# Expert layers of a two-block network on one core: overflow code out of line, transposes of half 0 ahead of the gate rows, one conditioning vector summed by column tiles

## The reference

```python
def layer_norm(x, g, b):
    mu = jnp.mean(x, -1, keepdims=True)
    var = jnp.mean(jnp.square(x - mu), -1, keepdims=True)
    return (x - mu) * lax.rsqrt(var + LN_EPS) * g + b
...
def moe_ffn(h, ...):            # 64 experts, 6 per token, one shared expert
    scores = jax.nn.sigmoid(xf @ router_w)
    ...                         # group-limited top 6, normalised gates topw
    routed = routed_experts(xf, topi, topw, w_gate, w_up, w_down)
    shared = (jax.nn.silu(xf @ sh_gate) * (xf @ sh_up)) @ sh_down
    return routed + shared
```

## Time and profile before

| | |
|---|---|
| time of three runs | 1858.17 us median (1858.16 to 1863.55) |
| the profiled execution: its own time, its span | 1860.38 us, 1858.6 us |
| mean granted TensorE clock in the span | 0.972 |
| busy: PE, PEld, DVE, ACT, POOL | 95%, 60%, 41%, 17%, 2% of the span |
| moved by DMA | 576.87 MB, mean 310 GB/s |

### The profile page before, as it was taken

One profiled execution on the slowest core, in us unless ns is written; L12 is line 12 of the kernel. 1 busy time (PEld: TensorE's weight loads), 2 busy tenths in 40 slices (PEclk: granted clock), 3 DMA queues, 4 the chain that ended last, 5 costly groups with the idle time before them and its releaser, 6 DMA issues.

```text
span 1858.6 us, 25707 instructions
## 1 busy us (share of the span) xinstructions
PE 1759.4 (95%) x10428; PEld 1109.3 (60%) x10428; DVE 756.0 (41%) x1545; ACT 307.6 (17%) x665; POOL 45.7 (2%) x86
## 2 busy tenths in 40 slices
PE   7999999999999979998999999999998699999998
PEld 3886754544444438887956544444443387778875
DVE  1667422222222225877764222222211366555173
ACT  1111300100000013431122101000000221320121
POOL 0110000000000000000000000000000000000000
PEclk7999899999999999999899999999999899999999
DMA  9978689999999975864386999999999765225301
GB/s 402 365 273 333 250 339 425 425 425 425 424 425 425 426 322 200 297 243 172 123 337 261 376 424 425 425 425 425 425 425 424 324 225 203 88 93 202 119 25 44
DMA packets 82099, 576.87 MB, mean 310 GB/s; under 512 B 9132, under 2 KB 11436, under 8 KB 12848
## 3 DMA queue, kind: packets, MB, share of 16 engines
q1 hardware_dynamic: 70992, 494.65, 64.8%
q0 software_dynamic: 10976, 80.43, 11.4%
HBM read 573.98 MB, written 1.06 MB: 309 GB/s over the span
## 4 chain that ended last, share of the span: by engine, by line
PE 63%; SPq 16%; DMA 15%; DVE 3%; issue 2%; ACT 0%; DVEq 0%; ACTq 0%
PE ps L339 62%; SPq L1465 14%; DMA wbuf<-in_moe_d 3%; DMA hma<-in_moe_gu 3%; DMA cst<-in_moe_gu 3%; DMA slab<-in_moe_gu 3%; DMA wbuf<-in_moe_gu 3%; PE ps L343 2%; SPq L1480 1%; DMA slab<-in_ada 1%; SPq L1475 0%; DVE hma L561 0%; DVE slab L3090 0%; DVE slab L3087 0%; DMA wbuf<-in_od_out 0%
## 5 line engine op out<-in xcount | busy, mean ns | idle before, releaser
L339 PE MATMUL ps<-slab 128*128 128x128 f32 (+8 forms) x3144 | 521.0, 354 | 22.3 <-DMA slab<-in_moe_gu 16.6
L339 PEld LDWEIGHTS ps<-slab 128*128 128x128 f32 (+4 forms) x3144 | 341.0, 174 | 192.7 <-issue 153.0
L339 PE MATMUL ps<-wbuf,slab 128*32 128x512 f32 (+3 forms) x1136 | 362.9, 603 | 8.2 <-DMA wbuf<-in_moe_gu 5.7
L339 PE MATMUL ps<-hma,wbuf 128*128 128x256 f32 (+2 forms) x1552 | 344.0, 383 | 2.6 <-DVE hma L351 2.6
L339 PEld LDWEIGHTS ps<-hma,wbuf 128*128 128x128 f32 (+1 forms) x1552 | 292.3, 193 | 50.1 <-issue 9.0
L339 PE MATMUL ps<-hma,slab 128*32 128x512 f32 (+2 forms) x504 | 197.4, 603 | 9.8 <-DMA hma<-in_moe_gu 9.8
L346 ACT ACTIVATE slab<-ps 128x256 f32<-128x256 f32 (+4 forms) x119 | 54.5, 470 | 899.8 <-PE ps L339 887.4
L339 PEld LDWEIGHTS ps<-wbuf,slab 128*32 128x32 f32 (+2 forms) x1136 | 111.7, 135 | 152.8 <-issue 130.7
L1708 DVE TENSOR_TENSOR slab<-ps,slab 128x256 f32<-128x256 f32 x44 | 18.7, 424 | 384.1 <-ACT slab L346 384.1
L339 PE MATMUL ps<-cst,slab 128*32 128x512 f32 (+6 forms) x500 | 161.1, 474 | 6.0 <-DMA cst<-in_moe_gu 6.0
L339 PE MATMUL ps<-slab,cst 128*32 128x512 f32 (+7 forms) x550 | 143.6, 550 | 5.4 <-ACT slab L346 5.3
(11 more groups left out here) (280 smaller groups left out, 1443.0 us busy)
## 6 DMA issues: line engine op xcount, KB each, us to landing
wbuf<-in_moe_gu SPq DMA_DIRECT2D x103, 1024.0 KB, 24.4
slab<-in_moe_gu SPq DMA_DIRECT2D x63, 1024.0 KB, 22.9
wbuf<-in_ada POOLq DMA_DIRECT2D x60, 1024.0 KB, 6.1
wbuf<-in_moe_d SPq DMA_DIRECT2D x57, 1024.0 KB, 25.2
hma<-in_moe_gu SPq DMA_DIRECT2D x49, 1024.0 KB, 24.2
slab<-in_moe_d SPq DMA_DIRECT2D x32, 1024.0 KB, 26.6
wbuf<-in_od_in SPq DMA_DIRECT2D x30, 1024.0 KB, 5.0
cst<-in_moe_gu SPq DMA_DIRECT2D x28, 1024.0 KB, 23.1
```

The lines of the kernel that those rows point to most:

```text
L339: return e.matmul(o, lhsT, rhs, start=start, stop=stop, skip_group_check=skip)
```

## The change

1. **Overflow code out of line** on PE, ACT and DVE; SP keeps the old form. The flag is loaded in block 10 of the 18 (`over_read`). Where the body stood there is now a branch on the flag to one of two labels. `..._some` holds one unconditional branch to the body, and `..._none` stands right behind it. The bodies stand near the end of each program, where the engine jumps over both (`over_bodies`): on PE behind its last product, on ACT and DVE ahead of the final statistics.
2. **The norms r0 and r1.** PE transposes half 0 first and then makes the gate rows, in banks 4 and 5. ACT copies the rows after its scaling of half 1.
3. **Conditioning vectors 7 and 15** are summed by column tiles: `ada_sum_pe` ahead of the router's logits, `ada_turn_pe` behind them, with `ada_row_act` in `res_act`. `ada_dve` moves out of `res_dve` to behind `router_dve`.
4. PSUM banks: the logits, the two shared tiles and the counts used banks 6, 7, 4, 5. Now the vector takes 7, the first three take 6, 4, 5, and the counts take bank 0.

```diff
         def res_pe(e, kind, last, rows=None, mid=None):
-            if rows is not None:
-                rows_pe(e, *rows)
             for m in range(2):
                 for f in range(2):
                     p = fill_bank(e, ("n_t", kind, m, f), ("n_x", kind, m, f), ("n_x" if last else "n_h", kind, m, f))
...
                     t.then_inc(*P.up("n_t", kind, m, f))
+                if m == 0 and rows is not None:
+                    ring = banks.ids, banks.i
+                    banks.ids, banks.i = [4, 5], 0
+                    rows_pe(e, *rows)
+                    banks.ids, banks.i = ring
...
         def res_dve(...)
             stats_dve(e, kind, 1)
             turned(0)
-            if mid is not None:
-                ada_dve(e, mid)
             centre(1)
             turned(1)
...
         def res_act(...)
             stats_act(e, kind, 0, eps5)
             centre(0)
-            if rows is not None:
-                rows_act(e, rows, g_rows, freed_by)
             stats_act(e, kind, 1, eps5)
...
                 turned(hT, "n_h", 1, 1, g1, b1)
+            if rows is not None:
+                rows_act(e, rows, g_rows, freed_by)
+            if ada is not None:
+                ada_row_act(e, ada)
             if scores is not None:
                 scores_act(e, scores)
...
         def moe_pe(e, l, h):
-            banks.ids, banks.i = [6, 7, 4, 5], 0
+            banks.ids, banks.i = [7], 0
+            ada_sum_pe(e, (7, 15)[l])
+            banks.ids, banks.i = [6, 4, 5], 0
...
             P.also("used", ("m_rt", l))
+            ada_turn_pe(e, (7, 15)[l])
...
+                if q == SHARED_AT:
+                    over_read(e, l, P)
...
-            over(e, l, over_pe, P)
+            over_past(e, l, over_pe, P)
...
         def moe_dve(e, l):
             router_dve(e, l)
+            ada_dve(e, (7, 15)[l])
...
+        def over_past(e, l, body, who):
+            name = f"m{l}_{who.name}"
...
+            here = nc.cur_bb
+            e.br_ne(over_flag[l, who.name], 0, f"{name}_some", f"{name}_none")
+            nc.switch_bb(f"{name}_some", parent=here)
+            e.br(f"{name}_far")
+            nc.switch_bb(f"{name}_none", parent=here.parent)
+            over_far.append((name, l, body, here))
+
+        def over_bodies(e, who):
...
+            e.br(f"{who.name}_rest")
+            for name, l, body, here in over_far:
+                nc.switch_bb(f"{name}_far", parent=here)
+                over_whole(e, l, body, who)
+                e.br(f"{name}_none")
+            nc.switch_bb(f"{who.name}_rest", parent=over_far[0][3].parent)
```

More of the change, by code:

```diff
@@ L580, in ada_load @@
             e.dma_start(ada_at(n, q), A["ada"][TASKS[n][0], q]).then_inc(*G.arrive(f"ada_w{(4 * n + q) % d}", ("ada", n, q)))
[L582 to L587, removed]
         def ada_sum_pe(e, n):
@@ L821, in res_pe, with res_act @@
             give_y()
-        def res_act(e, kind, last, rows=None, freed_by=(), scores=None):
+        def res_act(e, kind, last, rows=None, freed_by=(), scores=None, ada=None):
             g0, b0, g1, b1 = (comb[:, i, :] for i in range(4))
@@ L1489, in counts_pe @@
         def counts_pe(e, l):
+            banks.ids, banks.i = [0, 1, 2, 3], 0
             p = fill_bank(e, ("m_cnt", l), ("m_ord", l))
@@ L1681, in moe_act @@
                     gather_act(e, l, q + 1)
-            over(e, l, over_act, C)
+                if q == SHARED_AT:
+                    over_read(e, l, C)
+            over_past(e, l, over_act, C)
             e.preload_act_table_set(LN_EXP)
@@ L1725, in moe_dve @@
                     gather_dve(e, l, q + 1)
+                if q == SHARED_AT:
+                    over_read(e, l, V)
                 if q == 0:
@@ L1735, in moe_dve @@
                                     ALU.mult).then_inc(*V.up("m_ysc", l, q, f))
-            over(e, l, over_dve, V)
+            over_past(e, l, over_dve, V)
         o_wT = S(3, 2048)[0:64, 0:256]
@@ L1743, in build, with over_read, over_whole @@
         o_wv = S(1, 8, 256)[:, 4:6, :]
-        def over(e, l, body, who):
+        over_flag, over_far = {}, []
+        def over_read(e, l, who):
+            flag = over_flag[l, who.name] = e.alloc_register(f"m{l}_{who.name}_over")
+            e.wait_ge(*on("m_flag", l))
+            e.reg_load(flag, flags[0:1, l:l + 1])
+        def over_whole(e, l, body, who):
             L = f"m{l}"
             kept = who.now
[L1749 to L1759, removed]
-            who.now = kept
+            e.wait_ge(*on("m_y", l, NB - 1))
+            e.wait_ge(*on("m_ttc", l, NB - 1))
+            e.wait_ge(*on("m_ysc", l, NB - 1, 1))
+            body(e, L, l)
+            e.wait_ge(*on(L + "o_y", NE - 1))
+            e.wait_ge(*on(L + "o_h", NE - 1, 1))
+            e.wait_ge(*on(L + "o_w", NE - 1))
+            who.now = kept
@@ new lines, in over @@
+        def over(e, l, body, who):
+            over_read(e, l, who)
+            with e.If_ne(over_flag[l, who.name], 0):
+                over_whole(e, l, body, who)
+        def over_past(e, l, body, who):
+            name = f"m{l}_{who.name}"
+            if ev.dry:
+                over_whole(e, l, body, who)
+                return
+            here = nc.cur_bb
[4 more added lines that the diff above has]
+            over_far.append((name, l, body, here))
@@ L1762, in over_unit @@
+        def over_bodies(e, who):
+            if ev.dry:
+                return
+            e.br(f"{who.name}_rest")
+            for name, l, body, here in over_far:
+                nc.switch_bb(f"{name}_far", parent=here)
+                over_whole(e, l, body, who)
+                e.br(f"{name}_none")
+            nc.switch_bb(f"{who.name}_rest", parent=over_far[0][3].parent)
+            over_far.clear()
         def over_unit(x, w):
@@ L3021, in hyena_act @@
             e.preload_act_table_set(LN_EXP)
+            over_bodies(e, C)
             for m in range(2):
@@ L3096, in hyena_dve @@
             e.tensor_tensor(y_z[:, 0:6, :], y_z[:, 0:6, :], y_gt[:, 0:6, :], ALU.mult).then_inc(*V.up("y_g"))
+            over_bodies(e, V)
             def final(m, f):
@@ L3139, in pe_program @@
             even_pe(e)
-            res_pe(e, "r0", False, ("m0", mods[:, 5, :], ("mods", 5)), lambda: ada_pe(e, 7))
+            res_pe(e, "r0", False, ("m0", mods[:, 5, :], ("mods", 5)))
             moe_pe(e, 0, "r0")
@@ L3143, in pe_program @@
             delta_pe(e)
[L3144 removed]
+            res_pe(e, "r1", False, ("m1", mods[:, 11, :], ("mods", 11)))
             moe_pe(e, 1, "r1")
@@ L3148, in pe_program @@
             hyena_pe(e)
+            over_bodies(e, P)
         def act_program(e):
@@ L3152, in act_program @@
             even_act(e)
-            res_act(e, "r0", False, "m0", (("scaled", "e_out", 1),), 0)
+            res_act(e, "r0", False, "m0", (("scaled", "e_out", 1),), 0, 7)
             moe_act(e, 0)
@@ L3156, in act_program @@
             delta_act(e)
-            res_act(e, "r1", False, "m1", (("scaled", "d_out", 3),), 1)
+            res_act(e, "r1", False, "m1", (("scaled", "d_out", 3),), 1, 15)
             moe_act(e, 1)
@@ L3165, in dve_program @@
             even_dve(e)
-            res_dve(e, "r0", 0, 0, 0, 3, ALPHA, 7)
+            res_dve(e, "r0", 0, 0, 0, 3, ALPHA)
             moe_dve(e, 0)
@@ L3169, in dve_program @@
             delta_dve(e)
-            res_dve(e, "r1", 0, 1, 6, 3, ALPHA, 15)
+            res_dve(e, "r1", 0, 1, 6, 3, ALPHA)
             moe_dve(e, 1)
```

5 lines of the change are left out of this document (2 added, 3 removed).

## The result

The changed kernel takes **1833.94 us** (median of 4 executions, 1828.3 to 1837.59) against 1858.29 of the kernel before: a ratio of 0.9855, 95% interval [0.9836, 0.9875]. Run again (E9) it took 1835.27 (6 executions), ratio 0.9874 [0.9851, 0.9898]. By the medians the gain is 24.4 and 24.3 us, by the two ratios 27 and 23; 15.8 was forecast, and 1833.9 lies just under the range (1836 to 1849).

What follows compares the result with a forecast made beforehand. PE's products and the expert loads were taken to bound the kernel, both tied to each expert layer's start. Terms -5.7 - 3.9 - 0.7 - 0.7 - 4.8 = -15.8 us from 1858.2 gave 1842.4, range 1836 to 1849.

Steps and rivals of the forecast that it cites:

- Ends of the layers: Norms m0 and m1 behind the expert layers: a near branch costs nothing, gaining 5.7 us in layer 0, 3.9 in layer 1.
- the gap stays: Rival: the branch's price does not depend on its distance, so only r0 and r1 gain, 6.2 us, to 1852.0; chance 0.09.
- The aside that a late end of PE's branch would be hidden too: Layer 0, m0: if PE's branch still waited for its products, it would end at 686.0, hidden.
- Starts: Norms r0 and r1: new order and column-tile sum gain 0.7 us each, after 0.64 and 0.6 for added TensorE work.
- Clock in r0: TensorE stays at 2.4 GHz through r0's logits and shared products, gaining 4.8 us, in r0 alone.
- I count nothing: Norm m0: a clock gain of 3.0 us was kept as a bound only; m1 was given at most 2.
- Against it: r1 had the same gaps and no fall: Argument against the rival that the clock still falls in r0 (1847.2 us, chance 0.14).
- the clock recovers in m0 and m1 too: Rival: the clock also recovers in norms m0 and m1, another 3 to 5 us, about 1838; chance 0.17.
- The signs named: It would be wrong if PE's short branch showed microseconds, transposes behind the logits waited for ACT, or clock 0.50 turned up in new places.

Runs made afterwards that it cites:

- E9: The changed kernel run again without any change; 1835.27 us (6 executions), ratio 0.9874.
- E3: The changed kernel with the overflow body out of line on DVE alone, inline on TensorE and ACT; 1854.2 us, ratio 0.9970.
- E7: The changed kernel with the conditioning sum made again by eight one-column products, at its new place ahead of the logits; 1843.7 us, ratio 0.9909.
- E8: The changed kernel with the gate rows back ahead of the transposes on PE and at their old place on ACT; 1839.93 us, ratio 0.9899.
- E1: The kernel before with only the overflow bodies moved out of line on all three engines, norms as before; 1844.78 us, ratio 0.9922.
- E11: The kernel before with 128 already met waits added at TensorE's start, shifting its later code; 1860.91 us, ratio 1.0007.
- E10: The changed kernel with 128 already met waits added at TensorE's start, shifting its later code; 1834.69 us, ratio 0.9868.
- E4: The changed kernel with the overflow body out of line on TensorE alone, while DVE and ACT jump far; 1840.57 us, ratio 0.9905.
- E2: The changed kernel with the overflow bodies of all three engines inline, so the norm edits alone; 1852.67 us, ratio 0.9960.

## Why the prediction was wrong by 8 us, point by point

- **Ends of the layers, -5.7 and -3.9.** The trace has -5.6 and -3.9. That a near branch costs nothing was right (0.06 and 0.2 us), and the rival by which *the gap stays* is gone. By what the Trainium skill says ("Runtime: NRT & Kernel Launch", Instruction fetch mechanics), a taken branch whose target is not in the pages held must wait until the target's page is fetched. The trace agrees, with a packet of code behind each far jump (686.95 on DVE, 687.77 on TensorE) and none behind TensorE's near one at 674.3 until 691.96.
- **The aside that a late end of PE's branch would be hidden too** was wrong. It would hide in the kernel before, behind DVE's 5.68 us. In E3, where DVE goes on at once, PE itself stands 3.89 and then 1.18. Since the change removes both, it cost the forecast nothing.
- **Starts, -0.7 each.** They gave -1.4 and, in r1, -1.2 (with 0.4 lost among the experts behind). I had charged 0.6 for the transposes behind the logits; they cost 0.27. ACT's copy of the sum ended at 194.51, 1.3 us ahead of the transposes that wait for it (195.85), the margin worked out.
- **Clock in r0, -4.8.** Measured -4.8: from the logits to the counts 4.52 less, net of the 0.27 that the transposes add. The reason given was light products and idle together. In E7 the fall came back with the light products, in E8 with idle and the gate rows ahead, so either was enough there.
- **The step that failed is the term for the clock, -4.8 us "in r0 alone, since r1 had no fall", with "I count nothing" for m0 and nothing for m1 in the sum.** The one profile of before had no fall in r1 by luck. E1 and E11, with the same norms, have it: from r1's statistics to the counts they took 24.2 and 24.6 us, before 20.4, the changed kernel 19.2. The mean of the three is 3.9 above the changed kernel, where -0.7 was forecast. "Against it: r1 had the same gaps and no fall" was thus a reading of one execution.
- **The clock in m0 and m1** came back too, the rival *the clock recovers in m0 and m1 too*. From m0's first to its second transposes took 9.1 and 7.7 us with the old code (before, E11), and 8.0, 6.3 and 6.3 in the changed kernel (its profile, E9, E10): 1.5 less on average, and 2.7 in E9 against before, near the bound of 3.0 that the prediction left out of its sum. In m1, from the first transposes to the first projection, it is 19.0 and 19.3 against 18.0, 18.8 and 18.2: 0.8 less. This rival's 1838 was the nearest, and too narrow, because it left out r1.
- **The same over all executions.** (1 - granted clock) times the span has a mean of 55.6 us before (51 executions) and of 33.6 in E9; r0's stretch of 10.2 us at 0.50 is 5 of these. Over the 51 executions of before a microsecond of it goes with 0.42 us of time (correlation 0.82). By this rate, an estimate, the 17 us outside r0 are worth about 7.
- **A cost that I did not look for:** TensorE without code among the 64x64 products, 3.05 us in the profile of before, on average 1.7 more with the body inline than without. The "issue" rows at 858.26 and 872.58 stood in the chain, and I read only those beside the branches.
- The sum with what the runs showed: -5.6 - 3.9 - 1.4 - 4.8 for the ends, r0's order and its clock, -3.9 for r1, -1.5 and -0.8 for the clock in m0 and m1, -1.7 for the gaps: -23.6, against -24. Of these the norms' part, -10.1, is near the 10.8 between E1 and the changed kernel. Several terms are means of two or three profiles, so I don't take the fit for more than it is.
- **The signs named.** TensorE's short branch shows 0.2 us, and the transposes behind the logits did not wait for ACT. Rows at 0.50 did turn up in new places (834.8 to 838.2, 1380.9 to 1387.7), but such places differ between two executions of the changed kernel as well.
- **Left open:** why the clock falls in one execution and not in another of the same code, and whether it is the far jump of layer 0 that makes later packets of code late more often. The delta mixer behind m0's second transposes took 254.9 to 265.0 us over the 14 profiles. Without TensorE's gaps it is 262.0 and 257.4 in before and E11, and 263.6, 256.5 and 258.2 in the changed kernel, so no gain by the clock is shown there.

## What to carry to other kernels

Read a far jump by what it fetches and not by the branch's record: on DVE the record was 72 ns and the stop 5.7 us, and TensorE pays as DVE does, so that removing it on one of them alone uncovers the other (E3, E4). Look through the whole chain for "issue" on the engine that bounds, not only at the place of the edit. And where executions of one kernel spread by 10 us with the clock, price the idle that an edit removes by the clock too, with a range on the side of the gain. That a stretch kept its clock in one profile does not say that it keeps it in the next: profile the kernel before more than once.

## What the runs showed of the hardware

- Among the 64x64 products TensorE's packets of code (16 KB, 0.9 to 1.1 us for most) mostly followed each other every 3.3 to 5.1 us. The 15 that left PE without code came 5.6 to 9.4 us after the one before, in a 1 MB load or at its end. In all 26 gaps in m0, m1 and the delta mixer PE had instructions again 1.2 to 1.7 us after the packet's end.
- A far jump held TensorE's sequencer 3.7 us where next to nothing loads (1822.0, transfer engines 2% busy) and 6.0 to 7.4 amid loads; landing could need a second packet within ten products (E2, E3).
- The Trainium skill ("Advanced Engine Details and Errata", Control Flow Timing) gives about 108 ns for compare-and-branch. The near ones of the changed kernel took 45 to 72 ns on ACT and DVE and 205 to 237 on TensorE, half and twice that. For the far ones before, 6451 ns on TensorE and 5.68 us of idle behind a record of 72 ns on DVE, the measurement decides.
- In r0 the granted clock fell to 0.50 with 1.84 us of one-column products ahead (E7) and with the rows ahead and 1.91 us of idle (E8), one profile each; without both it did not fall in nine profiles. In r1 the same code fell or did not from one run to another: logits of 3.68 us in before, 6.93 in E1, 6.61 in E11.
